# Seven products in place of eight for two down layers of a fused fp32 network

## The reference

```python
def squared_relu_mlp(h, w_up, w_down):      # w_up: 1024 x 4096, w_down: 4096 x 1024
    a = jax.nn.relu(h @ w_up)
    return (a * a) @ w_down
...
h = h + squared_relu_mlp(rms_norm(h, ffn_norm[layer]), ff_up[layer], ff_down[layer])
```

## Time and profile before

| what | value |
|---|---|
| time, median of 3 runs | 2602.07 us |
| time of the profiled execution | 2599.2 us |
| its span, first to last instruction | 2597.4 us |
| mean granted TensorE clock, share of full | 0.965 |
| TensorE matmul busy | 2482.9 us, 96% |
| VectorE busy | 1411.5 us, 54% |
| ScalarE busy | 842.3 us, 32% |
| GpSimd busy | 261.2 us, 10% |

### The profile page before, as it was taken

How to read it: one execution, slowest core, us unless ns; L and a number is a source line. 1 busy time by engine, 2 the same in 40 slices (tenths; PEclk the granted TensorE clock), 3 DMA queues, 4 the chain that set the end, 5 groups by cost and what they waited for, 6 DMA issues and landing times.

```text
span 2597.4 us, 41258 instructions
## 1 busy us (share of the span) xinstructions
PE 2482.9 (96%) x17263; PEld 2249.7 (87%) x17263; DVE 1411.5 (54%) x1935; ACT 842.3 (32%) x1199; POOL 261.2 (10%) x203
## 2 busy tenths in 40 slices
PE   6999999999999999999999999999997899999998
PEld 6999999998999999999887888888994446988997
DVE  6777655654554344542565666677227464544543
ACT  4433444434321222322223222223223453422322
POOL 2000222323100000100111000002003100000001
PEclk9999999989999999999978999999997999999999
DMA  3222533335222222222102544543220000222221
GB/s 134 81 71 80 128 82 90 85 67 183 98 82 84 96 97 81 93 87 81 49 1 82 179 146 155 184 162 117 102 82 17 0 1 33 82 98 97 94 84 65
DMA packets 93881, 235.63 MB, mean 91 GB/s; under 512 B 60074, under 2 KB 61700, under 8 KB 69556
## 3 DMA queue, kind: packets, MB, share of 16 engines
q1 hardware_dynamic: 88208, 201.40, 23.4%
q10 hardware_dynamic: 5540, 32.30, 3.5%
HBM read 222.00 MB, written 11.67 MB: 90 GB/s over the span
## 4 chain that ended last, share of the span: by engine, by line
PE 87%; DVE 7%; ACT 3%; issue 2%; POOL 1%; DMA 1%; DVEq 0%; ACTq 0%; POOLq 0%; SPq 0%
PE ps L301 67%; PE ps L1121 1%; PE ps L1111 1%; PE ps L1135 1%; PE ps L305 1%; PE ps L2641 1%; PE ps L2659 1%; PE ps L1913 1%; PE ps L2649 1%; PE ps L1914 1%; PE ps L1148 1%; PE ps L1147 1%; ACT whi L317 1%; PE ps L1153 1%; DVE g_tmp L1335 1%
## 5 line engine op out<-in xcount | busy, mean ns | idle before, releaser
L301 PE MATMUL ps<-xa_hi,whi 128*128 128x264 f32 (+2 forms) x2944 | 653.9, 296 | 31.6 <-DVE wlo L324 20.2
L301 PE MATMUL ps<-xa_lo,whi 128*128 128x264 f32 (+2 forms) x2944 | 649.4, 295 | 0.0
L301 PE MATMUL ps<-xa_hi,wlo 128*128 128x264 f32 (+2 forms) x2944 | 648.8, 295 | 0.0
L301 PEld LDWEIGHTS ps<-xa_hi,whi 128*128 128x128 f32 x2944 | 468.4, 190 | 48.3 <-DVE wlo L324 22.4
L317 ACT ACTIVATE whi<-raw 128x2048 fp32r<-128x2048 f32 x161 | 307.4, 1909 | 558.8 <-PE ps L301 549.1
L301 PEld LDWEIGHTS ps<-xa_lo,whi 128*128 128x128 f32 x2944 | 467.2, 189 | 11.0
L301 PEld LDWEIGHTS ps<-xa_hi,wlo 128*128 128x128 f32 x2944 | 466.5, 190 | 10.8
L324 DVE TENSOR_TENSOR wlo<-raw,whi 128x2048 fp32r<-128x2048 f32 x161 | 370.1, 2299 | 185.3 <-ACT whi L317 182.6
L301 PE MATMUL ps<-xb_lo,whi 128*128 128x264 f32 (+1 forms) x1280 | 384.7, 341 | 0.0
L301 PE MATMUL ps<-xb_hi,whi 128*128 128x264 f32 (+1 forms) x1280 | 382.8, 340 | 1.8 <-DVEq L243 1.5
L301 PE MATMUL ps<-xb_hi,wlo 128*128 128x264 f32 (+1 forms) x1280 | 383.1, 340 | 0.0
(11 more groups left out here) (429 smaller groups left out, 2898.5 us busy)
## 6 DMA issues: line engine op xcount, KB each, us to landing
raw<-weights SPq DMA_DIRECT2D x161, 1024.0 KB, 4.8
mod_w<-weights_mod ACTq DMA_DIRECT2D x24, 1024.0 KB, 4.7
g_EC<-scr_g SPq DMA_DIRECT2D x10, 424.0 KB, 5.1
scr_z<-z_st SPq DMA_DIRECT2D x16, 264.0 KB, 4.5
g_D<-scr_g SPq DMA_DIRECT2D x10, 371.0 KB, 4.7
scr_a<-g_AT SPq DMA_DIRECT2D x10, 318.0 KB
h<-x_in ACTq DMA_DIRECT2D x4, 528.0 KB, 8.5
z_b<-scr_z SPq DMA_DIRECT2D x1, 2112.0 KB
```

Of the source, the lines that this page charges most:

```text
L301: mm = pe.matmul(ps[:, at_ + step * c + bank, 0:tn], w[:, hb.slot, k, c * P:(c + 1) * P], x[:, k, t0:t0 + tn], start=(k == 0 and n == 0), ...
```

## The change

The down layers of the first and the last MLP are computed as Strassen's method does, in its form with 7 products and 15 sums. In one half-block the 8 k-tiles are paired (even, odd) and so are the two tiles of output columns; the tokens are halved (264 or 256). The weight block is then a 2 x 2 matrix of quarters with 4 k-tiles x 128 columns each, the activations are a 2 x 2 matrix too, and seven products P1 to P7, each 4 k-tiles by 3 terms = 12 matmuls over 264 or 256 columns, give the four output quarters. VectorE makes four weight sums S1 to S4 for every half-block and the activation sums in the up layer. The output sums are made by leaving a product in PSUM, adding its bank to one quarter of `h`, letting the next product accumulate onto it, and adding the bank to another quarter.

```diff
+        def pe_product(pe, name, slot, bank, n, first=True, last=True, ready=None):
+            for q in range(KT // 2):
+                if ready: ready(q)
+                for m, (w, xs) in enumerate(((f_hi, fx_hi), (f_hi, fx_lo), (f_lo, fx_hi))):
+                    mm = pe.matmul(ps[:, bank, 0:n], w[:, slot, q, :], xs[:, x, q, 0:n], start=(first and q == 0 and m == 0),
...
+        def pe_fast_down(pe, f, hb, n):
...
+            for j in range(4):
+                x, start = F_BANK[j], j == 0
+                pe.wait_ge(S("dve_part"), f.low("P12", j))
...
+                pe_product(pe, "P1", f.slot(F_W["P1"]), x, n, last=False, ready=b_ready if start else None).then_inc(S("pe_part"), 1)
+                pe.wait_ge(S("dve_part"), f.low("P5", j))
+                if j:
+                    pe.wait_ge(S("two_ev"), f.tiles(7 + 2 * j))
+                pe_product(pe, "P5", f.slot(F_W["P5"]), F_Z, n, last=False, ready=b_ready if start else None).then_inc(S("pe_part"), 1)
...
+                pe_product(pe, "P2", f.slot(F_W["P2"]), F_Y, n, ready=c_ready if start else None).then_inc(S("pe_part"), 1)
+                if j:
...
+                    pe_product(pe, "P7", f.slot(F_W["P7"]), F_BANK[j - 1], n, first=False, last=False).then_inc(S("pe_part"), 1)
+                pe.wait_ge(S("dve_part"), f.low("P6", j))
+                pe.wait_ge(S("dve_out"), f.out("X1", j))
+                pe_product(pe, "P6", f.slot(F_W["P6"]), x, n, first=False, last=False, ready=t_ready if start else None).then_inc(S("pe_part"), 1)
+                pe.wait_ge(S("dve_part"), f.low("P3", j))
+                pe.wait_ge(S("dve_out"), f.out("Z5", j))
+                pe_product(pe, "P3", f.slot(F_W["P3"]), F_Z, n, first=False).then_inc(S("pe_part"), 1)
+                if j:
...
+                    pe_product(pe, "P4", f.last(j - 1), F_BANK[j - 1], n, first=False).then_inc(S("tiles_done"), 2)
...
+        def dve_fast_sums(dve, f, hb, j):
...
+            dve.tensor_tensor(f_sum[:, S1], a[1][0], a[1][1], ALU.add).then_inc(S("fast_sum"), 1)
+            dve.wait_ge(S("fast_sum"), f.sum("S1", j))
+            dve.tensor_tensor(f_sum[:, S2], f_sum[:, S1], a[0][0], ALU.subtract).then_inc(S("fast_sum"), 1)
+            dve.wait_ge(S("fast_sum"), f.sum("S2", j))
+            dve.tensor_tensor(f_sum[:, S4], a[0][1], f_sum[:, S2], ALU.subtract).then_inc(S("fast_sum"), 1)
...
+        def dve_fast_down(dve, f, hb, pieces, scale=None, low=None):
...
+            for j in range(4):
+                new, x = hb.after(j + 1), F_BANK[j]
+                if j < 3:
+                    dve_fast_sums(dve, f, new, j + 1)
+                dve.wait_ge(S("pe_part"), f.done("P1", j))
+                out(x, 2 * j, 0, "dve_out")
+                dve.wait_ge(S("pe_part"), f.done("P5", j))
+                out(F_Z, 2 * j + 1, 1, "dve_out")
+                if j < 3:
+                    dve_fast_sum(dve, f, j + 1, "P5", S1)
+                dve.wait_ge(S("pe_part"), f.done("P2", j))
...
+                out(F_Y, 2 * j, 0, "dve_out")
+                if j < 3:
+                    dve_fast_row(dve, f, new, j + 1)
+                if j:
...
+                    out(F_BANK[j - 1], 2 * j - 1, 1, "dve_out")
+                dve_fast_sum(dve, f, j, "P7", S3)
+                if j < 3:
+                    dve_fast_difference(dve, f, new, j + 1)
+                dve.wait_ge(S("pe_part"), f.done("P6", j))
+                out(x, 2 * j, 1, "dve_out")
+                if j < 3:
+                    dve_fast_sum(dve, f, j + 1, "P6", S2)
...
+                out(F_Z, 2 * j, 1, None if j else "two_ev")
+                if j < 3:
+                    dve_fast_sum(dve, f, j + 1, "P3", S4)
+                else:
+                    dve_split(dve, new)
+                if j:
+                    dve.wait_ge(S("tiles_done"), hb.index * 2 + 2 * j)
+                    out(F_BANK[j - 1], 2 * j - 1, 0, "two_ev", 2)
+                if j < 3:
+                    dve_fast_last(dve, f, new, j + 1)
+                if low and j:
+                    low((2 * j - 1, 2 * j))
...
+        def act_fast_up(act, f, hb, pieces, biased, func):
...
+                        act.activation(flat(m_y[:, c], pieces), flat(m_act[:, c], pieces), func, bias=m_act[:, c, N_META - 1:N_META])\
...
+                        act.activation(flat(m_y[:, c], pieces), flat(m_y[:, c], pieces), ACT.Square).then_inc(S("fast_y"), 1)
...
+                    act.activation(fast_b(fx_hi, c, j, n), cols(m_y[:, c], pieces), ACT.Copy).then_inc(S("two_hi"), 1)
...
+                act.activation(fx_hi[:, 4:7, j, 0:n], f_t[:, :, 0:n], ACT.Copy).then_inc(S("fast_xhi"), 1)
...
+        def dve_fast_up(dve, f, hb, pieces, biased):
...
+                    if biased:
+                        dve.tensor_tensor(cols(m_act[:, c], SHIFTED), pair(c, SHIFTED), cols(rstd, SHIFTED), ALU.mult).then_inc(S("two_ev"), 1)
+                        dve.wait_ge(S("fast_y"), f.count(8, t + 1 - 32))
...
+                    if c == 0:
+                        dve.tensor_tensor(y[0][1], y[0][1], y[0][0], ALU.subtract).then_inc(S("fast_x"), 1)
+                    else:
...
+                        dve.tensor_tensor(f_t[:, 0, 0:n], y[1][1], y[0][1], ALU.subtract).then_inc(S("fast_x"), 1)
+                        dve.wait_ge(S("fast_x"), f.ops(j, 2))
+                        dve.tensor_tensor(f_t[:, 1, 0:n], f_t[:, 0, 0:n], y[0][0], ALU.subtract).then_inc(S("fast_x"), 1)
+                        dve.tensor_tensor(f_t[:, 2, 0:n], y[1][0], f_t[:, 0, 0:n], ALU.subtract).then_inc(S("fast_x"), 1)
+                    dve.wait_ge(S("two_hi"), f.acts(t + 1))
+                    dve.tensor_tensor(fast_b(fx_lo, c, j, n), cols(m_y[:, c], pieces), fast_b(fx_hi, c, j, n).bitcast(F32), ALU.subtract)\
...
+                if j < 2:
+                    dve_split(dve, hb.after(j + 2))
+                if j == 1:
+                    dve_fast_sums(dve, f, hb.after(4), 0)
+                    dve_fast_difference(dve, f, hb.after(4), 0)
+                dve.wait_ge(S("fast_xhi"), f.pairs(j + 1))
+                dve.tensor_tensor(fx_lo[:, 4:7, j, 0:n], f_t[:, :, 0:n], fx_hi[:, 4:7, j, 0:n].bitcast(F32), ALU.subtract)\
...
+                if j == 2:
+                    dve_fast_row(dve, f, hb.after(4), 0)
+                    dve_fast_sum(dve, f, 0, "P5", S1)
+                    dve_fast_sum(dve, f, 0, "P6", S2)
+                elif j == 3:
+                    dve_fast_sum(dve, f, 0, "P3", S4)
+                    dve_fast_last(dve, f, hb.after(4), 0)
...
-                         pe_two_layers(pe, 2, HB_MLP0, 4, FULL, norm=1, sums=1),
+                         pe_two_layers(pe, 2, HB_MLP0, 4, FULL, norm=1, sums=1, fast=0),
...
-                         pe_two_layers(pe, 10, HB_MLP2, 4, LATE, norm=6, peel=True, sums=6, squared=("out_ev", 2 * KT + 2), up=SHIFTED),
+                         pe_two_layers(pe, 10, HB_MLP2, 4, LATE, norm=6, peel=True, sums=6, squared=("out_ev", 2 * KT + 2), up=SHIFTED, fast=1),
```

More of the change, by code:

```diff
@@ L570, in group, with pe_two_layers @@
+        def pe_two_layers(pe, base, first, groups, pieces, norm, peel=False, sums=None, squared=None, up=None, fast=None):
             def group(i, hb, start=False):
@@ L640, in group @@
             def group(i, hb, last=False):
+                if fast is not None:
+                    f = FastCounts(fast, i, base, first)
+                    dve_fast_up(dve, f, hb, halves(pieces), biased)
+                    dve_fast_down(dve, f, hb.after(4), halves(pieces), scale, last and scaled and
+                                  (lambda tiles: dve_scaled_low(dve, scaled[0], h, pieces, scaled[1], tiles)))
+                    return
                 for j in range(4):
```

291 lines of the change are left out of this document (248 added, 43 removed).

## The result

The changed kernel takes 2631.01 us, the median of 4 runs (2628.21 to 2631.78), beside 2602.57 us for the kernel before on the same chip (4 runs). The ratio is 1.0111, with a 95% interval from 1.0094 to 1.0129: 1.1% slower. The profiled execution spans 2630.0 us against 2597.4.

A forecast was written before the change was run, and what follows sets the result against it. TensorE's matmuls were taken to bound the kernel nearly everywhere. Terms -0.7 + 2.5 + 20 + 5.6, about +27.5 us on the profiled 2599.2, with 2.9 added for the median, gave 2630; range 2608 to 2650.

The forecast's parts named there:

- TensorE's saving: Down layers of first and last MLP: seven products remove 23.5 and 17.6 us, 41.1 us of TensorE's work.
- VectorE's steps: Middle down-layer steps: VectorE takes 9.4 and 9.7 us beside TensorE's 10.28 and 10.02, so it fits.
- Rival C: Down layers: small passes overlap nothing, so VectorE paces them; 98 and 101 us a group, 2669 us; chance 0.07.
- The hand-over of the first MLP: From up to down layer: TensorE idles 4.2 us before P6(0) awaiting the first addition to `h`; groups 93.0 against 94.0.
- The 0.6 at P5(1): First MLP's down layer: P5(1) waits 0.6 us because VectorE adds P3(0) late.
- The last group was to lose 3.5 more: First MLP's last group: also making `xa_lo` gives 3.5 us of further idle time, mostly before P6(2).
- The way into the mLSTM: End of first MLP: the mLSTM's second half-block is split late, 8.9 us after TensorE's end, needed at 5.9; +2.5 us.
- The last MLP: Up layer waits on ScalarE, VectorE arrives late, 8.9 us idle a group; groups 95.1 against 90.6 us.
- the +20: Last MLP in total: four groups +18, GpSimd's adds 2 more, shorter last addition 0.3 back; together +20 us.
- Rival B: Last MLP's up layer keeps pace, only the hand-over costs: +3.5, total 2607 without the clock, 2613 with; chance 0.10.
- The clock: After idles before P6(0) the granted clock falls to 0.50: +1.0 a group first MLP, +0.4 last, 5.6 us in all.
- Rival A: Whole change: VectorE is no hindrance, TensorE's list decides; 2561 us, faster; chance 0.10 including weaker forms at 2580 to 2595.

The follow-up runs named there:

- e_ceil: Changed kernel, VectorE's passes rearranged in both MLPs, with S2, S4 and rests of P5, P6, P3 cut to one column of 128 for pairs 1 to 3: 2577.0 us.
- e_plus2: Changed kernel with two more VectorE passes in the steps of the second and third tile pair of each down layer: 2661.5 us, ratio 1.0215.
- the filler: Changed kernel with 30 matmuls that nobody reads ahead of TensorE's wait for the first P6 in every group: 2625.0 us, ratio 1.0089.
- e_mlp2_only: Changed kernel with the seven products in the last MLP alone, first MLP as in the kernel before: 2625.7 us, ratio 1.0091.
- e_fill: Changed kernel with weight sums and rests put into VectorE's waits for ScalarE's square, last MLP only: 2628.0 us, ratio 1.0095.

## Why the prediction was right, and where it was off

The forecast was 2630, the median is 2631.01.

**TensorE's saving.** 41.1 us, as worked out. In e_ceil the first three down layers of the first MLP come within 2 us of the 41.1 that their products were reckoned at.

**VectorE's steps.** 9.4 us was put down for a middle step of the first MLP. S1 starts at 783.22 in one step and at 792.73 in the next, 9.5 us, and the passes start 0.60 to 0.61 apart, a dependent one 0.71 to 0.73 behind its source, as in the earlier trace rows. Rival C does not fit these rows: where nothing is waited for, a pass recorded with 0.68 us is followed after 0.60. The prediction read the section "The DRAIN you can't avoid" of the Trainium skill, page "VectorE: DVE Perf Modes", as a rule for every pass. The section goes on to say that an operation that is not held starts earlier, and with that these rows agree. By e_plus2 the room in a step is 0.2 us more than was reckoned.

**The hand-over of the first MLP.** Idle 4.2 us expected, 4.31, 4.31, 4.31 and 4.14 measured. The groups start 94.1, 95.0 and 93.7 us apart, 93.0 and 1.0 of clock expected. The 0.6 at P5(1) does not show, since P6 to P3 ran at low clock in the meantime; with the filler it does, 0.30. The last group was to lose 3.5 more: its down layer takes 50.7 us against 47.5 for the mean of the other three. **The way into the mLSTM is the term that was mis-sized**, 2.5 us expected, 1.1 measured. The rest of the second half-block is done 8.8 us after TensorE's last down product (8.9 expected), but it is needed 7.8 us after it and not 5.9: between the two half-blocks TensorE also has 24 matmuls of the norm's sums, 1.97 us in its timeline, which the walk left out. The row of TensorE's first matmul behind them:

```profile
1109.89 0.48 PE L316 MATMUL ps<-xa_hi,whi 128*128 128x264 f32 x2 [1.10 <-issue]
```

**The last MLP.** Idle 2.1, 1.0 and 4.6 us expected ahead of P1, P2 and P6; 1.93, 0.92 and 4.34 measured in its first group, 1.87, 0.93 and 4.38 in the second. VectorE's wait for ScalarE 1.52 expected, 1.45 to 1.61 measured. Groups start 95.4 us apart, 95.1 and 0.4 of clock expected. The 0.9 and 0.3 at P5(1) and P5(2) do not show; the first of them does with the filler, 0.62 to 0.79. The +20 and 4 times 0.4 compare with 22.9 by stage: 20.9 in the four down layers, 199.5 us in place of 178.6, and 2.0 in the first up layer, 39.7 us in place of 37.7. This second part is the stop of 1.75 us at 2265.99, which the walk does not have. Rival B falls with e_mlp2_only, and e_fill tests the cause: fill VectorE's waits, and P1 and P2 start on time.

**The clock.** 5.6 us expected. The filler gives back 3.7 by stage, 6.1 without the two places at which the clock fell anew, and 5.7 by ratio, none of them tight. Behind some of the eight stops the low clock lasted longer than the 3.4 us of the earlier trace rows: the two windows from 870 to 878 average 0.50 and 0.71, which is 6.3 us at half speed. Yet no more came back with the filler, so more of it than thought was hidden behind VectorE's backlog, and the two misses cancel.

**Rival A** gave 2561 if VectorE were no hindrance. e_ceil took away the better part of its weight work and came to 2577.

So the mechanism and the sum both hold, but some of the closeness is luck. The sum was made for a profiled execution, 2626.7 us, and the profiled one took 2631.8; 2.3 us of the difference lie ahead of the first MLP, where nothing changed. The 2.9 us put on for the median happened to cover most of it, while the changed kernel's median stands 0.8 below its profiled run. And the middle of the program moves by up to 13 us between profiles, more than any single term of the sum except the last MLP's.

## What to carry to other kernels

A trade of TensorE work for VectorE work has to be costed at the hand-over between stages and not only in the steady state: here every plain middle step had something to spare, and 34.5 of the 41.1 us saved went at the one point of each group where VectorE arrived with 8 us of passes in front of what TensorE needed. Putting the awaited pass ahead of the others moved the stop and hardly shrank it; what shrank it were passes taken off the engine, or put where it waits for somebody else. And where the state of the clock in an untouched stretch moves the total by as much as the edit does, compare the profiles stage by stage.
